# Expert rows weighted on the chip and added into the residual rows by an adding scatter, with a reordered router

## What is computed

```
h = h + concat(diff_attention, neighbourhood_attention) @ w_out      # h1
h = h + hier_moe(rms_norm(h, g_ffn), w_rg, w_re, w1, w3, w2)         # h2
h = h + rms_norm(p @ w_ple, g_ple) * sigmoid(rms_norm(h, g_plg) @ w_plg)

hier_moe(x): softmax over 4 groups, best group; softmax over its 8 experts, best two
    weights = g_gate * (e_w / sum(e_w)); experts = g_idx * 8 + e_i
    every token row goes to its two experts: ys = (silu(xb @ w1[e]) * (xb @ w3[e])) @ w2[e]
    out[token] += ys * weight
```

## Time and profile before

| What | Value |
|---|---|
| runs | 3491.36, 3491.62, 3495.02 us; median 3491.62 us |
| profiled execution | 3490.98 us, of which the span is 3489.2 us |
| busy in the span | PE 2927.1 us (84%), DVE 1540.2 (44%), ACT 1222.0 (35%), POOL 298.2 (9%) |
| mean granted clock of PE | 0.922 of full speed |
| router phase | first issue at 966.6 us |
| expert phase | first issue at 1084.1 us |
| ple_gate phase | first issue at 1693.3 us |
| HBM | 433.46 MB read, 107.79 MB written, mean 155 GB/s |

### The profile page before, as it was taken

How to read it: one execution, slowest core, us unless ns; L and a number is a source line. 1 busy time by engine, 2 the same in 40 slices (tenths; PEclk the granted TensorE clock), 3 DMA queues, 4 the chain that set the end, 5 groups by cost and what they waited for, 6 DMA issues and landing times. The chain is left out here.

```text
span 3489.2 us, 61320 instructions
## 1 busy us (share of the span) xinstructions
PE 2927.1 (84%) x22494; PEld 2278.4 (65%) x22494; DVE 1540.2 (44%) x2880; ACT 1222.0 (35%) x2193; POOL 298.2 (9%) x489
## 2 busy tenths in 40 slices
PE   7997875886966999999477999868877999868876
PEld 6785654665854888888365888754466888754455
DVE  3852666777222221222344421168844421058853
ACT  4332544666031110101243222258832222148841
POOL 0001641000002111111100000000000000000000
PEclk9998997898967999999788999979998999979988
DMA  5114543211346999999755222341044221160034
GB/s 181 66 72 162 136 129 105 63 35 65 99 147 225 386 394 393 392 394 395 249 189 175 94 96 72 121 141 34 10 157 160 103 99 72 66 205 19 25 121 163
DMA packets 246492, 541.80 MB, mean 155 GB/s; under 512 B 29904, under 2 KB 112656, under 8 KB 221680
## 3 DMA queue, kind: packets, MB, share of 16 engines
q1 hardware_dynamic: 216832, 460.21, 37.1%
q0 software_dynamic: 28544, 79.99, 6.9%
q10 hardware_dynamic: 1008, 0.20, 0.0%
HBM read 433.46 MB, written 107.79 MB: 155 GB/s over the span
## 5 line engine op out<-in xcount | busy, mean ns | idle before, releaser
L509 PE MATMUL ps<-in_wh,in_xh 128*128 (+1 forms) x1024 | 401.0, 392 | 0.0
L511 PE MATMUL ps<-in_wh,in_xl 128*128 (+1 forms) x1024 | 399.5, 390 | 0.0
L510 PE MATMUL ps<-in_wl,in_xh 128*128 (+1 forms) x1024 | 399.4, 390 | 0.0
L509 PEld LDWEIGHTS ps<-in_wh,in_xh 128*128 128x128 f32 x1024 | 193.1, 189 | 40.0
L510 PEld LDWEIGHTS ps<-in_wl,in_xh 128*128 128x128 f32 x1024 | 193.0, 188 | 39.8
L511 PEld LDWEIGHTS ps<-in_wh,in_xl 128*128 128x128 f32 x1024 | 192.8, 188 | 40.1
L1061 DVE TENSOR_TENSOR ex_hid<-ps,ex_act 32x128 f32<-32x128 f32 x96 | 28.2, 294 | 325.4 <-PE ps L1108 324.5
L509 PE MATMUL ps<-mix_in_wh,mix_in_xh 128*128 (+1 forms) x384 | 152.1, 396 | 9.0 <-DVE mix_in_out L426 5.4
L510 PE MATMUL ps<-mix_in_wl,mix_in_xh 128*128 (+1 forms) x384 | 149.9, 390 | 0.0
L511 PE MATMUL ps<-mix_in_wh,mix_in_xl 128*128 (+1 forms) x384 | 149.8, 390 | 0.0
L275 ACT COPY in_out<-ps 128x512 f32<-128x512 f32 x64 | 37.5, 587 | 249.0 <-PE ps L511 249.0
(11 more groups left out here) (408 smaller groups left out, 7318.9 us busy)
## 6 DMA issues: line engine op xcount, KB each, us to landing
ex_w_w1a<-in_w_dram SPq DMA_DIRECT2D x32, 1024.0 KB
ex_w_w1b<-in_w_dram SPq DMA_DIRECT2D x32, 1024.0 KB
ex_w_w3a<-in_w_dram SPq DMA_DIRECT2D x32, 1024.0 KB
ex_w_w3b<-in_w_dram SPq DMA_DIRECT2D x32, 1024.0 KB
ex_w_w2a<-in_w_dram SPq DMA_DIRECT2D x32, 1024.0 KB
ex_w_w2b<-in_w_dram SPq DMA_DIRECT2D x32, 1024.0 KB, 14.3
proj<-in_out SPq DMA_DIRECT2D x128, 256.0 KB, 2.0
da_w_ada<-in_w_ada_dram SPq DMA_DIRECT2D x32, 768.0 KB, 4.3
```

The lines of the kernel that those rows point to most:

```text
L509: pe.matmul(o, xh[:, kt, tok], wb[0], start=(kt == 0), stop=False)
L510: pe.matmul(o, xh[:, kt, tok], wb[1], start=False, stop=False)
L511: last = pe.matmul(o, xl[:, kt, tok], wb[0], start=False, stop=(kt == KT - 1))
```

## The change

Three things change together.

1. Weights. The router writes each slot's weight as a third column beside the token id and the row number (`tok`, `slot_rows` and `row` grow from 2 to 3 columns), and the row number is now the token's own row of h1. DVE multiplies the 96 result rows with it in SBUF, and POOL scatters them into h1 with an addition, so that h1 becomes h2 in place. Rows that only fill a block have the number of one of 128 extra rows behind h1, which the router writes once. `slot_y` and h2 are gone.
2. `ple_gate` has no mixing any more and is the common `dense_phase`; x is scaled in place.
3. Router. SP loads the x tiles, the first ahead of the gain and the router weights, which come as whole rows (`w_group`, `w_expert`) and are laid into a zeroed `wr` of 64 columns by POOL. PE now takes a 64-column piece of `wr` as stationary operand and 128 columns of the turned tile as moving operand, even pieces into the upper half of the partitions, odd pieces into the lower one; DVE copies the sum out (`lay_halves`), and one more product with a 0/1 matrix `fold` adds the halves and turns them. All `turn_p` but the first stand behind the logits. `weigh(1)` moves ahead of the table of blocks on DVE. POOL starts to scatter when the first half of the slots is ready.

```diff
-            for q in range(XB):
-                pool.dma_start(x[q][:], src[q * P:(q + 1) * P, :]).then_inc(x_loaded[q], 16)
+            for q in range(XB):
+                sp.dma_start(x[q][:], src[q * P:(q + 1) * P, :]).then_inc(x_loaded[q], 16)
+                if q == 0:
+                    sp.dma_start(gain_b[:], row_to_all(gain, DM)).then_inc(gain_loaded, 16)
+                    sp.dma_start(w_group[:], w_rg.rearrange("(p k) n -> p k n", p=P)).then_inc(weights_loaded, 16)
+                    sp.dma_start(w_expert[:], w_re.rearrange("(p k) n -> p k n", p=P)).then_inc(weights_loaded, 16)
...
+            pool.memset(wr[:], 0.0).then_inc(wr_cleared, 1)
+            pool.wait_ge(wr_cleared, 1)
+            pool.wait_ge(weights_loaded, 32)
+            pool.tensor_copy(wr[:, :, 0:N_GROUPS], w_group[:]).then_inc(wr_done, 1)
+            pool.tensor_copy(wr[:, :, N_GROUPS:NL], w_expert[:]).then_inc(wr_done, 1)
...
+            pool.dma_start(src[SEQ:SEQ + P, :], x[0][:]).then_inc(spare_h_written, 16)
...
+            def half_logits(t):
+
+                pe.wait_ge(x_out, t + 1)
+                if t >= 2:
+                    pe.wait_ge(half_out, t - 1)
+                for kt in range(KT):
+                    part = slice(kt % 2 * HALF, (kt % 2 + 1) * HALF)
+                    last = pe.matmul(psL[t % 2][part, :], wr[:, kt, :], xt[t % 2][:, kt * P:(kt + 1) * P], start=(kt < 2), stop=(kt >= KT - 2))
+                last.then_inc(halved, 1)
+
+            def join(t):
+
+                pe.wait_ge(half_out, t + 1)
+                pe.matmul(ps_logit[:, t * NL:(t + 1) * NL], halves[t % 2][:], fold[:], start=True, stop=True).then_inc(logits, 1)
+
             turn(0)
-            pe.wait_ge(weights_loaded, 32)
+            pe.wait_ge(wr_done, 2)
+            pe.wait_ge(consts_loaded, 16 * 7)
             for t in range(NT):
                 if t + 1 < NT:
                     turn(t + 1)
...
+                half_logits(t)
+                if t >= 1:
+                    join(t - 1)
+            pe.wait_ge(pr_loaded, 16)
+            turn_p(0)
+            join(NT - 1)
+            pe.wait_ge(l_taken, 1)
+            for i in range(1, NT // 2):
+                turn_p(i)
...
+            def lay_halves(t):
+                dve.wait_ge(halved, t + 1)
+                if t >= 2:
+                    dve.wait_ge(logits, t - 1)
+                dve.tensor_copy(halves[t % 2][:], psL[t % 2]).then_inc(half_out, 1)
...
+            for i in range(TOP_K):
+                dve.tensor_copy(tok[:, i, :, 2].bitcast(F), slot_w[:, i, :]).then_inc(weights_laid, 1)
...
-                pool.indirect_dma_start(out=k.slot_y[:, :], out_offset=bass.IndirectOffsetOnAxis(ap=row_own[:, 1:2], axis=0),
-                                        in_=y[:], in_offset=None).then_inc(stored, 16)
+                pool.indirect_dma_start(out=h[:, :], out_offset=bass.IndirectOffsetOnAxis(ap=row_own[:, 1:2], axis=0),
+                                        in_=y[:], in_offset=None, compute_op=ALU.add).then_inc(stored, 16)
...
-                dve.tensor_copy(y[:, 0:YM], psY[0:BR, 0:YM]).then_inc(y_out, 1)
+                dve.tensor_copy(y[:, 0:YM], psY[0:BR, 0:YM]).then_inc(y_copied, 1)
+
+                dve.wait_ge(y_copied, n + 1)
+                dve.wait_ge(row_loaded, 16 * (n + 1))
+                dve.tensor_scalar(y[:], y[:], row[:, 2:3].bitcast(F), None, ALU.mult).then_inc(y_out, 1)
...
-            mix(0, 0, 0)
             scale(0, 0)
...
-            mix(1, 1, 0)
             scale(1, 1)
```

More of the change, by code:

```diff
@@ L75, in dense_phase @@
 def dense_phase(nc, k, tag, src, w, dst, kinds, gain=None, shift=None, rope=None, head=None,
-                head_gain=None, resid=None, gate=None, times=None, order=None, after=None, turned=None, mixed=False):
+                head_gain=None, resid=None, gate=None, times=None, order=None, after=None, turned=None):
     C = len(kinds)
@@ L356, in scale @@
                     dve.wait_ge(x_rs, t + 1)
-                    if mixed and (not isinstance(t, int) or t > 0):
-                        dve.wait_ge(x_turned, t)
-                    last = dve.scalar_tensor_tensor(out=xs[p][:], in0=x[p][:], scalar=rs[:, one], in1=gain_b[:],
+                    last = dve.scalar_tensor_tensor(out=x[p][:], in0=x[p][:], scalar=rs[:, one], in1=gain_b[:],
                                                     op0=ALU.mult, op1=ALU.mult)
@@ L562, in router_phase @@
         xt = [s.sb(f"xt{p}", [P, DM]) for p in range(2)]
-        wr = s.sb("wr", [P, KT, NL])
+        HALF = P // 2
+        w_group, w_expert, wr = s.sb("w_group", [P, KT, N_GROUPS]), s.sb("w_expert", [P, KT, N_EXPERTS]), s.sb("wr", [P, KT, HALF])
+        halves, fold = [s.sb(f"halves{p}", [P, P]) for p in range(2)], s.sb("fold", [P, NL])
+        psL = [k.ps[:, 3 + p, 0:P] for p in range(2)]
+        wr_cleared, wr_done, halved, half_out = (s.sem(n) for n in ("wr_cleared", "wr_done", "halved", "half_out"))
         ss, ms, sd, rs = (s.sb(n, [P, NT]) for n in ("ss", "ms", "sd", "rs"))
@@ L728, in _ @@
                     turn(t + 1)
-                if t % 2 == 1:
-                    pe.wait_ge(pr_loaded, 16)
-                    turn_p(t // 2)
-                pe.wait_ge(x_out, t + 1)
-                for kt in range(KT):
-                    last = pe.matmul(ps_logit[:, t * NL:(t + 1) * NL], xt[t % 2][:, kt * P:(kt + 1) * P], wr[:, kt, :],
-                                     start=(kt == 0), stop=(kt == KT - 1))
-                last.then_inc(logits, 1)
+                half_logits(t)
[7 more added lines that the diff above has]
+                turn_p(i)
             pe.wait_ge(p_taken, NT // 2)
@@ L752, in _ @@
         def _(dve):
+            def lay_halves(t):
[3 more added lines that the diff above has]
+                dve.tensor_copy(halves[t % 2][:], psL[t % 2]).then_inc(half_out, 1)
             dve.wait_ge(gain_loaded, 16)
-            with dve.Fori(0, NT // XB) as j:
-                for q in range(XB):
-                    t = XB * j + q
-                    one = bass.ds(t, 1)
+            for t in range(NT):
+                    q, one = t, slice(t, t + 1)
                     dve.wait_ge(x_ss, t + 1)
@@ L863, in _, with expert_phase @@
                                    -3.0, None, ALU.add))
-            for t in range(1, NT):
+            for t in range(2, NT):
                 weigh(t)
-def expert_phase(nc, k, w1, w3, w2, after):
+def expert_phase(nc, k, w1, w3, w2, h, after):
     HK = KT // 2
@@ L884, in expert_phase @@
         wy = [s.sb(f"w_w2{n}", [P, HY, DM]) for n in "ab"]
-        idx, row, idx_own, row_own, nothing = (s.sb(n, [BR, 2], I32) for n in ("idx", "row", "idx_own", "row_own", "nothing"))
+        idx, row, idx_own, row_own, nothing = (s.sb(n, [BR, 3], I32) for n in ("idx", "row", "idx_own", "row_own", "nothing"))
         copied = s.sem("copied")
@@ L947, in hand_over @@
             def hand_over(of, to):
-                pool.tensor_tensor(to[:], of[:], nothing[:], ALU.add).then_inc(copied, 1)
+                pool.tensor_tensor(to[:, 0:2], of[:, 0:2], nothing[:, 0:2], ALU.add).then_inc(copied, 1)
                 pool.wait_ge(copied, 1)
```

130 lines of the change are left out of this document (51 added, 79 removed).

## The result

The changed kernel takes 3440.09 us (median of 4 runs, 3435.94 to 3441.09) against 3491.49 (4 runs, 3485.82 to 3495.02): a ratio of 0.9853, 95% interval 0.9841 to 0.9865. That is 51.4 us less, where the forecast of 3474 was 17 less than the profiled execution. The profiled execution took 3440.78 us, 50.2 less than that of before.

What follows compares the result with a forecast made beforehand. Taken as bounds: PE and DMA both full in the expert phase, DVE's mixing in ple_gate's loop, late weights in the router. 3491.0 - 40 (ple_gate) - 17 (router) + 33 (blocks) + 7 (expert end) = 3474 us; range 3438 to 3504.

Steps and rivals of the forecast that it cites:

- Router, start, -8: Router: PE turns the second tile at 981 instead of 989.03, once the constants have landed; 8 us saved.
- Router, logits, -9: Router up to the last logits: half products and join save 6 us, with three `turn_p` and their waits 9 us.
- 28 if ... PE holds its full clock: Upper bound of the router's saving of 17 us, if constants come by 978 and PE holds its full clock.
- Router, behind the logits, 0: Router after the logits: later rank and earlier `weigh(1)` cost nothing together, with 2 us either way.
- Expert phase, each block, 30 x 1.1 = +33: Expert phase: each adding scatter costs one transfer more, 1.1 us, in 30 blocks; 33 us longer.
- Expert phase, end, +7: Expert phase's closing chain: weighting and slower scatter landing enter twice, 3.5 us each; 7 us longer, bounds 2 and 10.
- ple_gate, -40: ple_gate without mixing: earlier start, five shorter periods and clock save 40 us, bounds 34 and 44.
- the five periods: ple_gate loop: five 13.0 us periods between squares each lose ACT's 4.15 us wait for DVE, 20.8 us.
- B: Expert phase: the addition's read is hidden, the period stays 18.2 us, the end costs 5; 3439 us, chance 0.22.
- C: Expert phase: each adding scatter costs 2.2 us a block, 66 us, and 10 at the end; 3510 us, chance 0.25.
- D: Router: PE still waits for constants until 989, saving 7 us instead of 17; 3484 us, chance 0.08.

Runs made afterwards that it cites:

- experiment 6: Kernel before with only the router's new loading (SP loads x first, weights as whole rows laid by POOL): 3487.28 us, ratio 0.9985.
- the plain scatter: Changed kernel with the adding scatter made a plain one, so residual and expert rows are not summed: 3414.09 us, ratio 0.9773.
- Experiment 3: Changed kernel with a second scatter of the same rows per block into an unread matrix: plain 3473.36 us, adding 3505.26 us.
- the last run: Changed kernel in which POOL still makes the 24 transfers of the old mixing in ple_gate while nobody mixes: 3466.83 us, ratio 0.9928.
- two variants: Changed kernel with one load of each block's table rows instead of two, 3445.64 us; the same with PE's second tile waiting for `fold` alone, 3444.48 us.
- whole logits: Changed kernel with the old logit products (turned tile stationary, 36 columns moving, no halves, no join): 3459.65 us, ratio 0.9912.

## Why the prediction was wrong, and where it was right

The direction, the signs of the main terms and the range held; the size did not. The forecast for the profiled execution was 3474 and it took 3440.78: 33.2 us apart. By the table of phases, the router gave 17.6 more, the expert phase took 17.1 less, ple_gate gave 0.4 more, and the rest took 1.9 more: 17.6 + 17.1 + 0.4 - 1.9 = 33.2.

- **Router, start, -8:** right, -9.0 (13.5 us behind the phase's start instead of 22.45). By itself it would have been worth 2.6 (experiment 6): the rest counts only because the turning of p, which waits for `pr`, moved too.
- **Router, logits, -9: the first step that failed.** It measured -22. I priced the half products as 2.3 us a tile, which is a price at the clock of before. At that clock they take 1.98 against 3.46, which is 1.5 a tile, near the 1.2 of the forecast. But at the full level, which seven of the eight tiles have, they take 1.09: another 6 us. And the seven turnings of the stretch take 9.0 us together instead of 13.2. These 10 us I had only as an end of the range ("28 if ... PE holds its full clock"), and with 34.6 the router passed even that. With the old products in the changed kernel PE is granted 0.50 and the phase is 18.6 us longer; that is shown. The p transposes in the stretch fell from 4.3 us to 0.6, and the waits for DVE's scaled tiles from 3.6 to 0.8, by the rows of the two timelines. The old products and the old places of `turn_p` don't add up: each put back alone costs over half of the 34.6 us (18.6 and 21.3), so how the gain splits between them is not shown.
- **Router, behind the logits, 0:** -3.6, outside my 2 us. `weigh(1)` is worth 3.8 of its own.
- **Expert phase, each block, 30 x 1.1 = +33: the second step that failed.** The mechanism is right: with the addition undone the block is short again, PE waits for weights, and nobody waits for the weighting. The term was too large: +0.61 a block against before, about +16.6 for all; 0.81 against the plain scatter. The reason that I gave for the term doesn't give it either: if a read is half of a transfer, one read more is half of 1.12, which is 0.56 and near the 0.61. That this fits is no proof, since the same addition cost 0.53, 0.81 and 1.12 elsewhere. My base of 18.2 us a block, from 22 issues in 400 us, was too coarse as well: it was 17.94.

  The step behind the term, that a transfer costs its busy share, failed for the loads: a transfer of 384 KB from HBM to SBUF costs 2.05 us of a block, one from SBUF to HBM 0.95, where the mean busy share of the earlier trace rows had given 1.12 for either. The rule in the Trainium skill, "Collectives: The Full Stack", section "The bandwidth ceiling: the fold count and why AG ≠ RS ≠ AR", is about collectives: a reducing transfer pays for two source reads, which halve its rate. Experiment 3 agrees, where the second adding scatter took 2.07 us against 0.95 for the second plain one; for the first scatter the addition cost less, 0.81.
- **Expert phase, end, +7:** right in size, +6.3. The weighting is worth 2.1 there and the addition 5.0, as forecast, but the landing grew by 1.3 us and not by 2 to 3.
- **ple_gate, -40:** right in size. The start gave 13.5 us where I had 15.3, the five periods 25.6 where the waits, `ye` and the clock made some 25, and the part behind the loop 1.3 where I had nothing. That DVE's waits alone were its price is not shown; the last run speaks for a share of the transfers.
- **The rivals:** B (hidden, 3439) met the time, but not by its reason. The read is not hidden, as the plain scatter's 3414 shows; the time fell near it by luck, because the router gave 17.6 more. C and D did not happen.

Open are the price of the addition by itself (0.53, 0.81 and 1.12 us in three surroundings), why a gather of fewer rows saves nothing, and the 15 us behind the last scatter in two variants.

## What to carry to other kernels

When a stretch is made of many short products, look at the granted clock of the stretch first and price an edit of its products at both levels: here another form of the products came with the other level, and with it everything else that PE did there became faster. Price a transfer in a full stream by adding the same transfer once more, and not by the busy share of its queue; loads and stores of one size differed by a factor of two (2.05 and 0.95 us, busy share 1.12). And when loads are put in another order, ask who stands in order behind the one that now comes last: the new loading was worth 2.6 us until that consumer was moved too.

## What the hardware showed beyond that

- With products of 36 moving columns between the turned tiles (whole logits), PE was busy without a gap from 986 to 1016 us and was granted 0.50 (1.2 GHz) in all of it. With products of 128 moving columns (the changed kernel), busy for 9.6 and 9.35 us of 10, it was granted 0.87 and then 1.00 (2.4 GHz).
- In the expert phase, a load of 384 KB beside the stream of weights cost 2.05 us whether indirect or direct, a store of as much 0.95. With the load the 16 DMA engines together moved less in a second, 361 GB/s instead of 378, with the store 382, at a busy share of 1.02 in all three.
- 32 of 96 rows left out of a gather on the average took 3 MB in 400 us from the queue's bytes, but under 1% from its packets and no time from the block.
